# A two-layer hybrid network on one core: its recurrent stage rebuilt around TensorE

## The reference, cut to what matters

```python
u = _dwconv(a * sigmoid(g), conv_w, conv_b)      # 31 taps, 512 channels, each channel by itself
u = silu(_layer_norm(u, ln_g, ln_b))
# mLSTM: 4 heads, forward and backward; context first, then the latent tokens with its final state
b = cumsum(log_f);  log_d[i, j] = b_i - b_j + log_i_j  for j <= i
m_row = max(log_inter, max_j log_d)
s = (q k^T) * exp(log_d - m_row)
h = (s v + inter * C q) / max(|sum_j s + inter * n q|, exp(-m_row))
hm = _rms(h_f + flip(h_b)) * head_gain * sigmoid(o)
y = concat(u, hm) @ w_out
```

## Time and profile before

| | |
|---|---|
| median of 3 runs | 4272.98 us (4269.17 to 4275.7) |
| the profiled execution | 4268.7 us |
| its span on the core | 4266.9 us |
| mean granted TensorE clock | 0.941 |
| busy: TensorE, VectorE, ScalarE, GpSimd | 92%, 41%, 35%, 34% |
| last QKVO chunk ends, first output chunk starts | 235.8 us, 681.2 us |

### The profile page before, as it was taken

One profiled execution on the slowest core, in us unless ns is written; L12 is line 12 of the kernel. 1 busy time (PEld: TensorE's weight loads), 2 busy tenths in 40 slices (PEclk: granted clock), 3 DMA queues, 4 the chain that ended last, 5 costly groups with the idle time before them and its releaser, 6 DMA issues.

```text
span 4266.9 us, 55864 instructions
## 1 busy us (share of the span) xinstructions
PE 3921.5 (92%) x20866; PEld 3121.7 (73%) x20866; DVE 1754.3 (41%) x2756; ACT 1514.7 (35%) x2541; POOL 1437.3 (34%) x644
## 2 busy tenths in 40 slices
PE   6957888999998799999997999999998999999998
PEld 4854556888887577778885777877886777886886
DVE  2794443523242455534434665232113556433112
ACT  3312224322123444433335555333224555433222
POOL 2669202332222100024442332333443223343443
PEclk9966768999999899999998999999999999999999
DMA  4313331211112000013231211222222112222222
GB/s 177 118 60 119 130 132 50 79 59 64 60 63 69 30 20 15 20 64 103 94 100 63 70 65 65 81 88 78 94 98 79 60 60 70 75 96 69 97 99 84
DMA packets 84555, 332.65 MB, mean 78 GB/s; under 512 B 9504, under 2 KB 9760, under 8 KB 77856
## 3 DMA queue, kind: packets, MB, share of 16 engines
q1 hardware_dynamic: 83664, 328.18, 22.5%
q10 hardware_dynamic: 720, 2.10, 0.1%
HBM read 328.14 MB, written 2.10 MB: 77 GB/s over the span
## 4 chain that ended last, share of the span: by engine, by line
PE 65%; issue 22%; POOL 8%; DVE 3%; ACT 2%; POOLq 0%; DVEq 0%; ACTq 0%
PE pB L281 13%; PE pB L283 12%; PE pB L1644 12%; PE pB L282 12%; POOL w_lo L2164 4%; POOL under L1104 2%; PE pO L1258 2%; POOL under L1106 2%; PE pS L413 2%; PE pB L1240 1%; PE pT L1250 1%; PE pS L1240 1%; PE pS L1674 1%; PE pT L1702 1%; PE pO L1724 1%
## 5 line engine op out<-in xcount | busy, mean ns | idle before, releaser
L2164 POOL TENSOR_TENSOR w_lo<-w_raw,w_hi 128x1024 fp32r<-128x1024 f32 x518 | 1261.8, 2438 | 2765.1 <-ACT w_hi L319 2764.8
L281 PE MATMUL pB<-h_hi,w_hi 128*128 128x512 f32 x2072 | 823.1, 397 | 46.6 <-POOL w_lo L2164 17.4
L282 PE MATMUL pB<-h_lo,w_hi 128*128 128x512 f32 x2072 | 812.9, 392 | 0.0
L283 PE MATMUL pB<-h_hi,w_lo 128*128 128x512 f32 x2072 | 812.2, 392 | 0.0
L319 ACT ACTIVATE w_hi<-w_raw 128x1024 fp32r<-128x1024 f32 x518 | 546.2, 1055 | 499.9 <-PE pB L283 330.0
L281 PEld LDWEIGHTS pB<-h_hi,w_hi 128*128 128x128 f32 x2072 | 394.3, 190 | 137.8 <-issue 48.7
L282 PEld LDWEIGHTS pB<-h_lo,w_hi 128*128 128x128 f32 x2072 | 394.0, 190 | 84.5 <-issue 4.3
L283 PEld LDWEIGHTS pB<-h_hi,w_lo 128*128 128x128 f32 x2072 | 393.6, 190 | 83.1
L281 PE MATMUL pB<-b_hi,w_hi 128*128 128x512 f32 (+1 forms) x1112 | 421.4, 379 | 16.1 <-DVE xb_lo L700 10.3
L282 PE MATMUL pB<-b_lo,w_hi 128*128 128x512 f32 (+1 forms) x1112 | 409.2, 368 | 0.0
L283 PE MATMUL pB<-b_hi,w_lo 128*128 128x512 f32 (+1 forms) x1112 | 409.0, 368 | 0.0
(11 more groups left out here) (399 smaller groups left out, 5658.3 us busy)
## 6 DMA issues: line engine op xcount, KB each, us to landing
w_raw<-stream SPq DMA_DIRECT2D x518, 512.0 KB, 3.3
under<-ada SPq DMA_DIRECT2D x42, 1024.0 KB, 4.8
arena<-ada SPq DMA_DIRECT2D x6, 1024.0 KB, 17.3
x<-xT SPq DMA_DIRECT2D x1, 2048.0 KB, 10.4
out<-x SPq DMA_DIRECT2D x8, 256.0 KB, 2.0
xc<-cT SPq DMA_DIRECT2D x1, 1024.0 KB, 10.6
arena<-bmask ACTq DMA_DIRECT2D x1, 1024.0 KB, 4.8
arena<-brope ACTq DMA_DIRECT2D x2, 256.0 KB, 5.2
```

Of the source, the lines that this page charges most:

```text
L281: pe.matmul(dst, lh, rh, start=(begin and k == 0), stop=False)
L282: pe.matmul(dst, lh, rl, start=False, stop=False)
L283: last = pe.matmul(dst, ll, rh, start=False, stop=(end and k == len(pairs) - 1))
L2164: pool.tensor_tensor(w_lo[:, s, :], w_raw[:, s, :], w_hi[:, s, :].bitcast(F32), ALU.subtract).then_inc(lo_ready, 1)
```

## The change

The 16 gates become a weight chunk of their own (two groups of 8 columns at 0 and 32), the first of 13 QKVO chunks per stream; the two small gate weight tiles go. The steps from the gates to the running maxima are spread between the context's QKVO chunks: the gate rows are turned by small products, and the maxima are taken along rows for all heads and directions at once. VectorE builds, after the latent QKVO chunks, a table with the 31 taps of each channel as 32x32 diagonal blocks. The convolution is done by TensorE: 31 taps by 4 channel blocks, tap `k` in column part `k % 4`, block `r` in row part and PSUM bank `r`; ScalarE and VectorE copy two banks each, and four products with `stack` add the four partial sums. GpSimd's and VectorE's taps go. The layer norms come between the convolution and the scans, but for their split, which comes after. In the scans the scores are computed transposed, key tile by key tile, so that nothing is turned; each scan keeps six accumulators in the two banks of `pB`, and divides once at its end. A modulation load and its turns are spread over all 48 steps. The first two output chunks run together, input tile by input tile, as these become ready.

```diff
-G_QKVO = [_take(12), _take(12)]
+G_QKVO = [_take(13), _take(13)]
...
+        def pe_gates(pe, i):
+            if i == 1:
+                pe.wait_ge(*ev(G_QKVO[0]))
+                pe.wait_ge(*ev(G_QKVO[1]))
                 for d in range(2):
+                    r = slice(32 * d, 32 * d + 8)
+                    for p, t in enumerate(ORDER[d]):
+                        o = d * 512 + p * 8
+                        last = pe.matmul(pS[:, o:o + 8], grow[r, t * P:(t + 1) * P], ident[r, r], start=True, stop=True)
+                last.then_inc(gates_sum, 1)
+            elif i == 3:
+                pe.wait_ge(logf_ready, 1)
+                b4 = pS[:, 512:560].rearrange("p (d t h) -> p d t h", d=2, h=HEADS_M)
+                f4 = ga.rearrange("p (d t e) -> p d t e", d=2, e=2 * HEADS_M)[:, :, :, HEADS_M:]
+                for d in range(2):
+                    pe.matmul(b4[:, d], const(("upto", "from")[d]), f4[:, d], start=(d == 0), stop=False)
+                for k in range(1, 6):
+                    last = pe.matmul(b4[:, :, k:6, :], ones, f4[:, :, 0:6 - k, :], start=False, stop=(k == 5))
+                last.then_inc(prefix_sum, 1)
+            elif i == 5:
+                pe.wait_ge(u_ready, 1)
+                pe.matmul(pS[0:24, 0:P], u_[:, 0:24], ident, start=True, stop=True)
+                pe.matmul(pS[32:56, 0:P], u_[:, 24:48], const("flip"), start=True, stop=True).then_inc(u_rows, 1)
+            elif i == 7:
+                pe.wait_ge(prefix_max, 7)
+                pe.matmul(pS[0:1, 512:568], prefix[1][:, 191:192], ident[0:56, 0:56], start=True, stop=True).then_inc(tile_max, 1)
+            elif i == 8:
+                pe.wait_ge(carried, 1)
+                pe.matmul(pS[0:56, 0:1], carry, ones[0:1, 0:1], start=True, stop=True).then_inc(carry_turned, 1)
+            elif i == 10:
...
+        def dve_diag(dve):
...
+            dve.wait_ge(chunk_done, done(G_QKVO[0] + 12))
+            for j in range(CT):
+                w = pc[:, _cols["conv_w"] + j * TAPS:_cols["conv_w"] + (j + 1) * TAPS]
+                dve.tensor_tensor(diag[j].rearrange("p (k m) -> p k m", m=32), stack.unsqueeze(1).broadcast_to([P, TAPS, 32]),
+                                  w.unsqueeze(2).broadcast_to([P, TAPS, 32]), ALU.mult).then_inc(diag_ready, 1)
...
+        def pe_conv(pe, x):
+            s, j = CONVS[x]
+            n = NTOK[s]
+            pe.wait_ge(conv_ca, x)
+            pe.wait_ge(conv_cd, x)
+            pe.wait_ge(diag_ready, j + 1)
+            for k0 in range(0, TAPS, 4):
+                for c in range(min(4, TAPS - k0)):
+                    k = k0 + c
+                    for r in range(4):
+                        b = slice(32 * r, 32 * r + 32)
+                        last = pe.matmul(cbank[r][32 * c:32 * c + 32, 0:n], diag[j][b, 32 * k:32 * k + 32], up[s][b, j, k:k + n],
+                                         start=(k0 == 0), stop=(k + 4 >= TAPS))
+            last.then_inc(conv_done, 1)
...
+        def pe_conv_sum(pe, x):
+            s, j = CONVS[x]
+            n = NTOK[s]
+            pe.wait_ge(conv_ca, x + 1)
+            pe.wait_ge(conv_cd, x + 1)
+            if x >= 2:
+                pe.wait_ge(conv_out, x - 1)
+            for r in range(4):
+                last = pe.matmul(pB[32 * r:32 * r + 32, x % 2 * 512:x % 2 * 512 + n], stack, cpart[x % 2][r][:, 0:n], start=True, stop=True)
+            last.then_inc(conv_sum, 1)
...
+        def dve_conv(dve, x):
+            n = NTOK[CONVS[x][0]]
+            dve.wait_ge(conv_done, x + 1)
+            if x >= 2:
+                dve.wait_ge(conv_sum, x - 1)
+            for r in range(2, 4):
+                last = dve.tensor_copy(cpart[x % 2][r][:, 0:n], cbank[r][:, 0:n])
+            last.then_inc(conv_cd, 1)
...
+        ITEMS = [("N", 0)]
+        for _q in range(SCANS):
+            for _kt in range(6):
+                if _kt == 3 and _q % 2 == 0 and _q:
+                    ITEMS.append(("F", _q // 2 - 1))
+                if _kt == 5 and _q + 1 < SCANS:
+                    ITEMS.append(("N", _q + 1))
+                ITEMS.append(("S", 6 * _q + _kt))
+        ITEMS.append(("F", HEADS_M - 1))
...
+        def pe_values_step(pe, m):
+            q, kt = divmod(m, 6)
+            d, h = q % 2, q // 2
+            pe.wait_ge(ml_p, m + 1)
+            if kt == 0:
+                if q:
+                    pe.wait_ge(ml_ev, q)
+                else:
+                    pe.wait_ge(conv_out, len(CONVS))
+            began = set() if kt == 0 else {0, 1}
+            for a, b in queries(d, kt):
+                for t in range(a, b):
+                    p = place(d, t)
+                    last = pe.matmul(acc[:, p // 3, p % 3, :], expo[m % 3][:, t * P:(t + 1) * P], v_at(kt, h),
+                                     start=(p // 3 not in began), stop=((kt, t) == last_into(d, p // 3)))
+                    began.add(p // 3)
+            last.then_inc(ml_pv, 1)
...
+        def pe_mlstm(pe):
+            pe.wait_ge(padded, 1)
+            pe.wait_ge(ncm_ready, 1)
+            for i in range(10, 13):
+                pe.wait_ge(*ev(G_QKVO[1] + i))
+            pe.wait_ge(vm_copied, 2 * HEADS_M)
+            for x in range(len(CONVS)):
+                pe_conv(pe, x)
+                if x:
+                    pe_conv_sum(pe, x - 1)
+                if x == CT + 1:
+                    pe_ln_mean(pe, 0)
+                if x == CT + 3:
+                    pe_ln_squares(pe, 0)
+            pe_conv_sum(pe, len(CONVS) - 1)
+            pe_item(pe, ("N", 0))
+            pe_ln_mean(pe, 1)
+            pe_item(pe, ("S", 0))
+            pe_ln_squares(pe, 1)
+            pe.wait_ge(rt_ready, NORMS.index("ln_ctx") + 1)
+            at = ITEMS.index(("S", 0)) + 1
+            for m in range(STEPS):
+                while m + 1 < STEPS and at <= ITEMS.index(("S", m + 1)):
+                    pe_item(pe, ITEMS[at])
+                    at += 1
+                for k in range(ADA_FIRST, n_ada):
+                    if ada_step(k) == m:
+                        pe_ada_late(pe, k)
+                for g in ada_groups_at(m - 2):
+                    pe_ada_turn_late(pe, g)
+                pe_values_step(pe, m)
+            for m in (STEPS, STEPS + 1):
+                for g in ada_groups_at(m - 2):
+                    pe_ada_turn_late(pe, g)
...
+        def pe_about(pe):
+            g = G_ABOUT[0]
+            pe.wait_ge(ml_ev, SCANS)
+            for e in range(2):
+                pe_wait_chunk(pe, g + e)
+            for kt in range(KD):
+                if kt == CT:
+                    pe_item(pe, ("F", HEADS_M - 1))
+                if kt < CT:
+                    pe.wait_ge(nlo_ready, N_OUT[NORMS.index("ln_lat")] + kt + 1)
+                else:
+                    pe.wait_ge(hs_lo, 2 * (kt - CT) + 2)
+                for e in range(2):
+                    s = (g + e) % SLOTS
+                    last = pe_three(pe, bank[s][:, 0:T], [(wt(s, kt), rows(*H, T, kt, 0, T))], kt == 0, kt == KD - 1)
+                    if kt == KD - 1:
+                        last.then_inc(chunk_done, 1)
...
+        def act_bias_rows(act, q):
+            act.wait_ge(ml_n, q + 1)
+            if q >= 2:
+                act.wait_ge(ml_e, 6 * (q - 1))
+            act.activation(nbig[q % 2], half_of("N", q)[:, 0:TC], ACT.Copy).then_inc(ml_nb, 1)
+        def act_weights(act, m):
+            q, kt = divmod(m, 6)
+            d, h = q % 2, q // 2
+            act.wait_ge(ml_nb, q + 1)
+            act.wait_ge(ml_nd, q + 1)
+            if m >= 3:
+                act.wait_ge(ml_pv, m - 2)
+            c = gcol(d, kt, h)
+            runs = [(ndiag, kt, kt + 1)]
+            for a, b in queries(d, kt):
+                runs += [(nbig, r0, r1) for r0, r1 in ((a, min(b, kt)), (max(a, kt + 1), b)) if r0 < r1]
+            for src, r0, r1 in runs:
+                last = act.activation(expo[m % 3][:, r0 * P:r1 * P], src[q % 2][:, r0 * P:r1 * P], ACT.Exp, bias=u_[:, c:c + 1])
+            last.then_inc(ml_e, 1)
...
+        def dve_bias_diag(dve, q):
+            dve.wait_ge(ml_nb, q + 1)
+            dve.tensor_tensor(ndiag[q % 2].rearrange("p (a b) -> p a b", b=P), nbig[q % 2].rearrange("p (a b) -> p a b", b=P),
+                              const("mask_b" if q % 2 == 0 else "mask_f").unsqueeze(1).broadcast_to([P, 6, P]), ALU.add).then_inc(ml_nd, 1)
+        def dve_weighted(dve, m):
+            q, kt = divmod(m, 6)
+            dve.wait_ge(ml_s, m + 1)
+            dve.wait_ge(ml_e, m + 1)
+            for a, b in queries(q % 2, kt):
+                pk = expo[m % 3][:, a * P:b * P]
+                last = dve.scalar_tensor_tensor(pk, half_of("S", m)[:, a * P:b * P], QK_M ** -0.5, pk, ALU.mult, ALU.mult)
+            last.then_inc(ml_p, 1)
+        def dve_scan_end(dve, link, q):
+            d, h = q % 2, q // 2
+            hs = hflat[h % 2].rearrange("p (a b) -> p a b", b=P)
+            dve.wait_ge(ml_pv, 6 * q + 6)
+            dve.wait_ge(guard_ready, 1)
```

(31 more changed lines are left out.)

701 lines of the change are left out of this document (361 added, 340 removed).

## The result

The changed kernel takes 4113.11 us (median of 4 runs, 4109.69 to 4119.67) against 4273.07 us for the kernel before: a ratio of 0.9628, 95% interval 0.9616 to 0.964. The profiled execution took 4109.69 us with a span of 4107.9 us. The forecast was 4112 us for the median and 4108 us for the profiled execution. The total is right; two of its larger terms are not, and they cancelled.

A forecast was written before the change was run, and what follows sets the result against it. Bound by a 445.4 us stage: a 53 us TensorE wait and scans at clock 0.70. Terms 8.4 + 7 + 56 + 26 + 178 + 9.4 = 284.8 gain 160.6: 4108 profiled, 4112 median, range 4080 to 4140.

The forecast's parts named there:

- Gates: Two added gate weight chunks at 8.4 us, plus gate steps between context chunks at 7 us.
- Convolution: Eight tiles of 31 taps on TensorE, with copies, form changes and the latent mean: 56 us.
- full overlap: Convolution on TensorE: all sixteen 32x32 parts work at once, 6.7 us per latent tile, 3.3 per context tile, together 40.
- the rival of issue at 0.05: Convolution tiles bound by issue: 1984 pairs take 99 us, 59 more than 40, total 4171 us; chance 0.13.
- latent tile of 10 us or more: Convolution: sign that the forecast is wrong and issue binds the tiles.
- End of the norms: Chain from the last convolution tile through norms and SiLU to the first weights and product: 26 us.
- Scans: Eight scans: 158 us of TensorE work, 12 of seam waits, 8 for a cold start, sum 178 us.
- seam waits: Between scans, 1.5 us stays uncovered before the next scan's first value product: 12 us in all.
- After the scans: First two output chunks with the last head's chain: 18.5 to 20 us against 11, 9.4 us more.
- The clock did not stay at 0.70: Rival for the scans: mean clock stays 0.70, so 238 us, 60 more, total 4172 us; chance 0.2.
- little overlap: Rival for the convolution: pairs at 0.1225 us, 243 us in all, 203 more, total 4315 us; chance 0.05.
- signs of being right: Convolution matmuls every 0.027 us, some 50 us; scans 20 to 22 us, clock above 0.9, no idle above 3 us.

The follow-up runs named there:

- the run with the late SiLU: Changed kernel with both streams' SiLU and the table load behind it moved into the second scan's third step: 4100.09 us, 0.9594 of the kernel before.
- the transposes: Changed kernel with the earlier kernel's 168 TensorE transposes of weighted blocks added back to the scans, read by nobody: 4127.64 us.
- the pauses: Changed kernel with TensorE also waiting for chained ScalarE copies at the seven seams between scans: 4117.03 us with two copies, 4151.41 us with five.
- the version of both: Changed kernel with SiLU late and the last convolution tile's copies and sum put between the latent norm's second and third square: 4098.79 us, 0.9591 of before.

## Why the prediction was right, and where its terms were not

*Gates.* Forecast 8.4 + 7 = 15.4 us, measured 14.1. Between the context chunks TensorE waits 0.2 us in all for the gates' chain, and the 53.2 us wait is gone. This part held.

*Convolution.* Forecast 56 us (its terms, 4 x 8.4 + 4 x 4.5 + 3.4, add up to 55), measured 72.4 (249.9 to the last matmul at 322.3). This is the step that failed: "So I take full overlap", drawn from 32 pairs in a row. In a run of 1984 pairs a pair costs 0.031 us with 512 columns, where I had 0.027 (6.7/248), and 0.027 on average with 256, where I had 0.0133 (3.3/248). Doubling the matmuls added 57.3 us where full overlap is 40. It is a mis-sized term, not the rival of issue at 0.05, and the sign of being wrong "latent tile of 10 us or more" is not met by the matmuls (8.65) but is by the period (10.04, 1.39 of it for the copies, forecast within 1.7). The Trainium skill (TensorE: Matmul & The Clock Gate, Measured speedup vs the span model) gave an estimated 60 us by its 10.6-fold overlap. The 57.3 us are nearer to that than to my 40, but in part by chance: the figure is for 512 columns, and there the tiles overlap more (248 x 0.43/7.67, 13.9-fold), while the context tiles, for which it was not given, overlap less. Its 62 ns per matmul in microcode (same page, Wait — 56ns, not 53.3ns?) I had applied to each record pair, which gave 123 us. One matmul instruction here is two records, and so costs 0.062 us in latent tiles, the same number; but the 124 of the first context tile took 5.76 us (292.18, 1.39 us behind the copies at 290.79, to 297.94), 0.046 each, so it is not a floor here.

*End of the norms.* Forecast 26 us, measured 24.8 (322.3 to 347.06). The chain ran as counted, with the SiLU and its table loads last. The forecast priced it and did not ask whether it had to stand there: it did not, and the run with the late SiLU takes 7.5 us from it.

*Scans.* Forecast 178 us, measured 165.9 (347.06 to the last value step's end at 513.0). The forecast had 158 us of work, 12 of seam waits and 8 for a cold start. The work was right, although its score term is 0.5 us a scan too high (21 blocks at 1.49 us for 6 are 5.2 and not 5.7). At the high clock a scan takes 19.9 and 21.7 us in turn (VectorE's reciprocals at the ends, 411.99, 431.88 and 453.55 us). With the first at 17.7, as in the run with the late SiLU, six such in turn and the last at 16.9 (496.71 to 513.58), it comes to 159.3. The seam waits were wrong: score, broadcast bias and ada products cover the scaling, and TensorE does not wait there. The other 7 us (166.5 from 347.06 to 513.58, less 159.3) are the clock's: 4.1 in the first scan (21.8 instead of 17.7), half of the 8 forecast, and two short falls of 1.6 us that were not forecast. The first fall lies in this window, in which TensorE had no idle at all:

```profile
366.00:387.00 21.00, 21.00 (x133) 12.84 (x133) 8.14 (x15) 6.64 (x15) 0.00 (x0) 0.92 0.71 254
```

What made the scans 160 us shorter (325.9 to 165.9) can be split only by an estimate. TensorE idled 65 us in them before (325.9 - 260.6) and 3 us now (168.00 - 164.57), which is 62; the transposes are 16; at the high clock the work of before would be some 175 us (159 + 16), so of its 260.6 busy us some 85 were the low clock's, against 7 now. The transposes and the pauses were tried by runs. Which part of the rebuilding (the maxima moved out, one division per scan, the order of the keys) took away which waits was not.

*After the scans.* Forecast 9.4 us more than two dense chunks, measured 8.5 (513.0 to 532.5, less 11). Held.

Together 14.1 + 72.4 + 24.8 + 165.9 + 8.5 = 285.7 against 284.8: the convolution's 16.4 us too few were made up by 12.1 too many in the scans and 3.4 in the rest. That the sum came within 1 us is luck, since the two misses have nothing to do with each other. The gain of 159.0 us (4268.7 to 4109.7) is that of the forecast, 160.6, but not for all of its reasons.

*The rivals.* The clock did not stay at 0.70; the pauses show that seams that idle would have brought it part of the way there, to 0.80. Issue at 0.05 us and little overlap did not occur: 0.031 is far from 0.10, from which the change would not have gained. The 0.045 us that spoke for issue was misread: its 40 pairs hold 8 on the whole array, and the 16 small ones by themselves took 0.36 us (2381.11 to 2381.47), 0.0225 each. Of the signs of being right, scans of 20 to 22 us at a clock above 0.9 and no long waits in them came true; matmuls every 0.027 us and a convolution of some 50 us did not.

## What to carry to other kernels

Price idle of TensorE by what it does to the clock: here 14.5 us in seven short waits cost 41 us. Ask of each chain that ends on the critical path whether all of its parts are needed there; a result that is first read 170 us later, such as the SiLU's (343.5 and 514.0 us), can be made beside the scans. Small parts of the array overlap well, but a short burst in a trace did not give the rate of a long run; a doubled copy of the loop did.

## What the runs showed that was not expected

- With eight of the 16 parts at work (two row groups) the granted clock stood at 0.50 though TensorE was busy for 15.70 of 15.70 us; half the convolution took longer than all of it, and the kernel 27.3 us more by the spans. With twelve parts it was 1.00.
- Inside the scans the clock fell at seams without any idle ahead of it. By windows of 4 us of the changed kernel:

```profile
363.00:367.00 4.00, 4.00 (x27) 2.45 (x26) 1.16 (x2) 2.11 (x5) 0.00 (x0) 1.00 0.66 242
367.00:371.00 4.00, 4.00 (x19) 2.08 (x22) 3.09 (x7) 1.31 (x4) 0.00 (x0) 0.81 0.59 244
371.00:375.00 4.00, 4.00 (x28) 2.03 (x20) 1.22 (x3) 0.69 (x2) 0.00 (x0) 0.77 0.36 119
375.00:379.00 4.00, 4.00 (x33) 2.57 (x29) 0.99 (x2) 0.80 (x2) 0.00 (x0) 1.00 0.91 344
```

It happened at two of the seven seams of this execution, behind the first and the fifth scan, and cost about 1.6 us each time (21.46 us between the ends of two scans instead of 19.89). Ahead of it stood turns with 2 moving columns and products on half the rows. That these bring it was not tried, and they can't be all of it: the same instructions stand ahead of the seam behind the third scan (408.90 to 411.49 us), where the clock stayed at 1.00. A second execution of the changed kernel had its falls behind the first and the seventh scan, and that of the version of both only behind the seventh.

- A long run of 32x32 parts has gaps of up to 1.3 us that the profile puts down to issue, 3.4 us in the convolution and 10.0 with the matmuls doubled. What makes them is open. From 249 to 330 us one of the DMA queues carried 16 packets of instructions (0.26 MB); whether the gaps wait for them was not tested.
